# Down weights of experts 2 to 15 requested behind the next expert's gate/up weights, as the later ones are

## What is computed

```python
logits = xn @ w_router + b_router
top_val, top_idx = lax.top_k(logits, 4)
gates = softmax(top_val)
# for every expert e, for the tokens that chose it:
hgu  = xb @ w_gate_up[e] + b_gate_up[e]          # 1024 -> 2048
g, u = min(hgu[:, :1024], 7), clip(hgu[:, 1024:], -7, 7)
hact = (u + 1) * (g * sigmoid(1.702 * g))
out  = hact @ w_down[e] + b_down[e]              # 1024 -> 1024, times its gate, added to its tokens
```

## Time and profile before

| | us |
|---|---|
| median of 3 runs | 1267.32 |
| lowest, highest | 1266.35, 1267.43 |
| the profiled execution | 1267.62 |
| its span, first to last instruction | 1265.8 |

### The profile page before, as it was taken

The page is one execution under the profiler, slowest core; times in us unless marked ns, Lnnn a source line. Parts: engine busy times, 40 slices in busy tenths (PEclk is TensorE's granted clock), DMA queues, the critical chain, the costliest instruction groups (busy, mean ns, idle before and its releaser), DMA issues.

```text
span 1265.8 us, 18432 instructions
## 1 busy us (share of the span) xinstructions
PE 1187.5 (94%) x7503; PEld 612.4 (48%) x7504; DVE 479.3 (38%) x742; ACT 250.5 (20%) x353; POOL 5.4 (0%) x11
## 2 busy tenths in 40 slices
PE   8999999999899999999999899999999898999996
PEld 7999998998533333333333333333333333333332
DVE  6867867654423232222223222222223222222223
ACT  5439544544410100001000000001000100000002
POOL 0000100000000000000000000000000000000000
PEclk9999999999999999999999999999999999999999
DMA  8525745544999999999999999999999999999995
GB/s 327 196 100 200 246 163 202 180 152 161 423 419 428 429 430 427 429 429 428 428 428 430 427 428 430 430 427 429 429 429 427 428 430 428 427 430 430 427 428 241
DMA packets 36832, 461.28 MB, mean 364 GB/s; under 512 B 4272, under 2 KB 4416, under 8 KB 5568
## 3 DMA queue, kind: packets, MB, share of 16 engines
q1 hardware_dynamic: 36288, 460.16, 87.3%
q0 software_dynamic: 224, 0.54, 0.1%
q10 hardware_dynamic: 288, 0.12, 0.0%
HBM read 459.76 MB, written 1.05 MB: 364 GB/s over the span
## 4 chain that ended last, share of the span: by engine, by line
PE 50%; DMA 48%; DVE 1%; issue 1%; ACT 0%; SPq 0%; DVEq 0%
DMA late<-in_w_gate_up 44%; PE ps L1294 21%; PE ps L1159 6%; PE ps L1160 5%; PE ps L1161 5%; DMA s<-in_w_down 3%; PE ps L1180 2%; PE ps L1178 2%; PE ps L1179 2%; PE ps L1194 2%; PE ps L1346 1%; PE ps L1320 1%; PE ps L1354 1%; DMA raw<-in_dense 1%; PE ps L1247 1%
## 5 line engine op out<-in xcount | busy, mean ns | idle before, releaser
L1294 PE MATMUL ps<-late,s 128*64 128x512 f32 x1128 | 513.9, 598 | 58.7 <-DMA late<-in_w_gate_up 57.1
L1295 PE MATMUL ps<-late,s 128*64 128x512 f32 x1128 | 513.9, 598 | 0.0
L1294 PEld LDWEIGHTS ps<-late,s 128*64 128x64 f32 x1128 | 143.4, 136 | 382.7 <-issue 259.5
L1044 DVE TENSOR_TENSOR res<-res,ps 128x1024 f32<-128x1024 f32 x64 | 78.2, 1221 | 248.9 <-PE ps L1346 241.5
L1159 PE MATMUL ps<-act_hi,whi 128*128 128x256 f32 x576 | 164.3, 285 | 3.9 <-DVE act_lo L703 2.3
L1160 PE MATMUL ps<-act_lo,whi 128*128 128x256 f32 x576 | 163.6, 284 | 0.0
L1161 PE MATMUL ps<-act_hi,wlo 128*128 128x256 f32 x576 | 163.6, 284 | 0.0
L619 ACT ACTIVATE s<-ps 128x512 f32<-128x512 f32 x64 | 34.7, 594 | 558.5 <-PE ps L1295 558.5
L1295 PEld LDWEIGHTS ps<-late,s 128*64 128x64 f32 x1128 | 143.4, 136 | 0.0
L722 DVE TENSOR_TENSOR wlo<-raw,whi 128x2048 fp32r<-128x2048 f32 x47 | 107.3, 2289 | 52.4 <-ACT whi L452 52.3
L1294 PE MATMUL ps<-raw,s 128*64 128x512 f32 x272 | 123.8, 598 | 0.2
(11 more groups left out here) (184 smaller groups left out, 972.6 us busy)
## 6 DMA issues: line engine op xcount, KB each, us to landing
late<-in_w_gate_up SPq DMA_DIRECT2D x125, 2048.0 KB, 25.5
raw<-in_w_down SPq DMA_DIRECT2D x31, 2048.0 KB, 25.6
raw<-in_dense SPq DMA_DIRECT2D x51, 1024.0 KB, 4.9
late<-in_w_down SPq DMA_DIRECT2D x16, 2048.0 KB, 25.3
s<-in_w_down SPq DMA_DIRECT2D x16, 2048.0 KB, 25.3
raw<-in_w_gate_up SPq DMA_DIRECT2D x2, 2048.0 KB, 9.5
s<-in_w_gate_up SPq DMA_DIRECT2D x1, 2048.0 KB, 12.2
raw<-in_w_down SPq DMA_DIRECT2D x2, 1024.0 KB, 34.0
```

The costliest lines, as they stand in the source:

```text
L1044: V.tensor_tensor(res[:, t, :], res[:, t, :], ps[:, OUT_BANK[t]:OUT_BANK[t] + 2, :].rearrange("p b n -> p (b n)"), ALU.add)\
L1294: nc.tensor.matmul(ps[0:SLOTS, bank, :], x_tile, lower, start=start, stop=stop)
L1295: return nc.tensor.matmul(ps[SLOTS:P, bank, :], x_tile, upper, start=start, stop=stop)
```

## The change

`SHIFT` goes from 7 to 0, and the first loop, which would have no step left, is taken out. The calls behind it have `SHIFT` in their numbers and so begin at expert 1:

```diff
-SHIFT = 7
+SHIFT = 0
@@
-                with sp.Fori(0, SHIFT) as i:
-                    for half in range(2):
-                        e = i * 2 + (1 + half)
-                        next_gate_up(e)
-                        for jj in range(DN_CHUNKS // 2):
-                            used(r, e, GU_CHUNKS + 2 * jj + 1)
-                            load_down(r, i + 1, half, jj)
                 next_gate_up(2 * SHIFT + 1)
                 next_gate_up(2 * SHIFT + 2)
                 for jj in range(DN_CHUNKS // 2):
                     load_down(r, SHIFT + 1, 0, jj)
                 with sp.Fori(SHIFT + 1, EXPERTS // 2 - 1) as i:
```

## The result

| | before | after |
|---|---|---|
| median of the runs taken beside each other | 1267.35 us (1266.22 to 1267.61) | 1270.55 us (1270.26 to 1271.32) |
| profiled execution | 1267.62 | 1271.29 |
| its span | 1265.8 | 1269.5 |

The changed kernel takes 1.0028 of the time before, 95% interval 1.0021 to 1.0036: 3.2 us more. A ratio of 1 lies well outside the interval, so the loss is small but real.

A forecast was written before the change was run, and what follows sets the result against it. The prediction took the expert stage to be bound by a never-dry queue of weight transfers. A 2.4 us hole plus 0.8 us for an instruction load gave +3.2 on the median 1267.32: 1270.5 us, range 1268.8 to 1272.8.

The forecast's parts named there:

- The bound: Expert stage, 395 to 1251 us: a transfer queue that never runs dry, 4.89 us per 2 MB transfer, then a fixed tail.
- The 175 behind it take 175 x 4.893 = 856.3: Transfers behind expert 2's first down request, which lands at 395.2, run without a hole and end at 1251.5 us.
- The hole: No request from 376.87 to 390.03; expert 3's first gate/up load lands at 397.6, not 395.2: 2.4 us lost.
- The surcharge: Instruction load at 393.6 shows after the engines start level behind the gap: 0.8 us, bounds 0 and 1.3.
- the row at 350.34: Transfer in the kernel before, landing at 360.9 with two instruction loads in 356 to 360; 1.3 us lost, taken as upper bound.
- The sum: Whole kernel: 2.4 + 0.8 = +3.2 us, all reaching the end, on the median 1267.32 gives 1270.5 us.
- (a): Rival, first transfer behind the gap: instruction load falls on an engine with time to spare; 1269.4 to 1269.7 us, chance 0.22.
- (b): Rival, request at 390.03: fixed time shrinks on just-busy engines, under 1 us lost; 1267.3 to 1268.3 us, chance 0.07.
- (c): Rival, three requests behind the gap: a shallow queue loses 1.3 us on each; +6.3, 1273.6 us, chance 0.10.
- The fixed part: Alternative estimate at the gap: about 2.0 us fixed per DMA makes it 1.6 us; 1268.9 us without the 0.8.
- theory L: Experiments' theory: a fresh start takes 7.6 us and levels the 16 engines; 1.8 us extra is an instruction load on one.

The follow-up runs named there:

- the run with one early step: Changed kernel with the early-order loop run once, so down requests of experts 2 and 3 go out early; 1267.59 us, ratio 1.0002 to the kernel before.
- the kernel with counters: Changed kernel with 120 counter instructions at the head of TensorE's program; 1288.61 us, against 1284.63 us for the kernel before with the same counters.
- the hole at 834: Changed kernel with SP waiting once, ahead of expert 18's gate/up requests, until all requested loads have landed; 1274.77 us, ratio 1.0058 to the kernel before.

## Why the prediction was right, and where it was off

**The bound.** The step from the chain of waits to "The 175 behind it take 175 x 4.893 = 856.3", with no hole among them, held: with the hole added, the last weights land 3.7 us later in the profiled execution, and its time is 3.7 us more. That nothing is paid for the order itself is shown by the run with one early step and by the 29.36 us.

**The hole.** Its place was right to half a microsecond: no request from 376.4 to 389.5. Its time from the rows of lone transfers, 7.6 us, was 0.3 short for a lone transfer (7.9 in three runs), and that the queue sets the landings behind it held too.

**The surcharge was mis-sized.** I took 0.8 us with an upper bound of 1.3 and said 7.6 to 8.9 us to landing; it was 9.4, a surcharge of 1.8. The step that was off is the bound: the row at 350.34 shows what one such place cost, and I used it as the most that an instruction load can cost. The runs have 8.7, 8.8, 8.9 and 9.4 with a load on its way, 7.9 without.

The traces show the shape of it as well. The semaphore of such a load counts sixteen steps. Behind the hole of the changed kernel fifteen of them have come 7.5 us after the request and the last after 9.4; in the other three with an instruction load fifteen have come by 7.6 to 7.7 and the last by 8.7 to 8.9; in the two without, by 7.5 and 7.9. So one part of the sixteen is held up, by 0.8 to 1.5 us over the 7.9; the instruction load's packet itself takes 0.9. Why it is 1.5 in one execution wasn't found.

The trace of the kernel before had two more such places that I didn't use: with instruction loads in 338 to 346, the loads requested near 328.4 and 328.75 land after 14.5 and 19.9 us, 5.3 and 5.7 behind the one ahead in place of 4.9, in a queue that wasn't empty.

**The sum.** 1270.5 was forecast and 1270.55 measured, closer than its terms deserve; that the two agree to 0.05 us is luck. The hole in the profile is 4.3 us, not 3.2. Of this 0.6 was won ahead of it: the landing ahead is at 389.7, before it was at 390.3, most of this because the down load requested at 350.11 lands after 10.3 us, where the earlier trace rows has 10.6, so that the place which lost 1.3 us before loses 0.8 in this execution. That leaves 3.7 between the profiled executions; the medians are 3.2 apart. The profiled execution of the changed kernel is the second slowest of ten, 0.7 us over their median, so the last half microsecond fits the spread of single executions. What the surcharge is in the others isn't known.

**The rivals.** (a) fell with the 9.4. (b) fell most clearly: the fixed part didn't shrink for a request 0.2 us ahead of the last landing, nor in the kernel with counters, with no instruction load near, for one 0.1 us ahead of it (407.31, landing at 407.4; 7.9 us). (c) had a true core, a loss of 0.7 to 0.8 us on the second transfer behind a near-empty queue in two of the experiments; in the changed kernel the second lands 398.9 to 403.8 = 4.9 behind the first and loses nothing.

**The fixed part.** The estimate from the fixed part of about 2.0 us per DMA of the Trainium skill, "DMA: Bandwidth & Descriptors", section "Anatomy of one DMA — SWDGE (gpsimd) path", was 1268.9. That section's fit is for DMAs issued by GpSimd. Those here are issued by SP, and their rows decide: a lone 2 MB load takes 7.6 to 7.9 us, 2.7 to 3.0 over its share of a full queue. On the instruction loads the Trainium skill, "Runtime: NRT & Kernel Launch", section "Instruction fetch mechanics", says that a sequencer fetches its next block by a DMA queue of its own and that the cost of crossing into that block is mostly hidden. It gives no cost for the data transfers beside such a load. Of those the landings here show that nothing was lost in the deep queue of the kernel before (400.2 and 405.0 in step), and 0.8 to 1.5 us over a lone transfer's 7.9 right behind a hole.

## What to carry over

Where a chain of waits shows transfers released by a compute engine and the engine released by transfers, count the transfers between two landings: if the count times the period fits, the queue is full, and an edit to the order of requests costs what holes it opens. Look for such holes where the queue is shallow, at the start of the stage: write down request times and landings, take out the moved request, and see whether the next request still comes a lone transfer's fixed time (here 3 us) ahead of the last landing. While the transfers stay the bound, as they did here, a hole isn't made up for behind it, and what is saved ahead of it is lost.

## What was not expected of the hardware

- An instruction load of 16 KB on its way with the first transfer behind a hole moved its landing from 7.9 to between 8.7 and 9.4 us after the request, though its bytes are under 1% of the 2 MB. In the deep queue 0.9 us was lost where one was listed at 1222 to 1225, the first load of that size behind the hole at 834; in the kernel before the one at 392 to 395 cost nothing.
- From the first to the last of a load's sixteen semaphore steps it takes 2.3 us in the deep queue before and 2.0 in the last load ahead of the hole after, but 1.0 and 0.9 in the first load behind a hole where no instruction load is on its way. That is the levelling which theory L supposed; that it is the reason why an instruction load shows there fits every row, but no run changed it by itself.
- With requests 4.0 us apart on an empty queue and no instruction load on its way, the second transfer landed 5.7 us behind the first; with requests 0.5 us apart, 4.9. The cause stays open.
- 120 counter instructions at the head of TensorE's program delay its first matmul by 17.5 us, about 0.15 us each.
